# MLP input of a gMLP layer: the two transpositions left on TensorE go to VectorE, by k-tiles, from quadrants moved within SBUF

## The reference

```python
x = x + gmlp_mixer(rms_norm(x, norm1_g), a_w_in, a_ln_g, a_ws, a_bs, a_w_out)
x = x + channel_mlp(rms_norm(x, norm2_g), mlp_w1, mlp_w2)    # square(relu(h @ w1)) @ w2
return rms_norm(x, final_g)
```

## Time and profile before

| | |
|---|---|
| median of 3 runs | 1124.3 us (1124.18, 1124.3, 1125.67) |
| the profiled execution's own time | 1126.03 us |
| its span, first to last instruction | 1124.2 us |
| PE busy | 1114.8 us, 5088 matmuls |
| DVE busy | 785.9 us, 833 instructions |
| ACT busy | 569.4 us, 870 instructions |
| POOL busy | 23.5 us |
| mean granted clock of PE | 0.998 |
| DMA | 193.80 MB, mean 172 GB/s |

### The profile page before, as it was taken

How to read it: one execution, slowest core, us unless ns; L and a number is a source line. 1 busy time by engine, 2 the same in 40 slices (tenths; PEclk the granted TensorE clock), 3 DMA queues, 4 the chain that set the end, 5 groups by cost and what they waited for, 6 DMA issues and landing times.

```text
span 1124.2 us, 13090 instructions
## 1 busy us (share of the span) xinstructions
PE 1114.8 (99%) x5088; PEld 928.2 (83%) x5088; DVE 785.9 (70%) x833; ACT 569.4 (51%) x870; POOL 23.5 (2%) x17
## 2 busy tenths in 40 slices
PE   8999999999999999999999999999999999999997
PEld 7888888888888888888888888888888888888886
DVE  4976655688779986678658547455599575677666
ACT  6774444553554334565774365454653433433456
POOL 0000000000000000000000000000000000000240
PEclk9999999999999999999999999999999999999999
DMA  8173253272865494731353635527878354343213
GB/s 294 45 210 127 94 187 113 75 244 93 316 250 221 159 358 144 217 113 38 113 187 126 211 113 183 193 108 272 293 292 305 111 226 187 113 150 113 78 73 150
DMA packets 81933, 193.80 MB, mean 172 GB/s; under 512 B 4528, under 2 KB 10704, under 8 KB 75216
## 3 DMA queue, kind: packets, MB, share of 16 engines
q1 hardware_dynamic: 81392, 192.69, 48.7%
q10 hardware_dynamic: 480, 0.28, 0.1%
HBM read 134.24 MB, written 58.72 MB: 172 GB/s over the span
## 4 chain that ended last, share of the span: by engine, by line
PE 98%; DMA 1%; ACT 0%; DVE 0%; ACTq 0%; issue 0%
PE banks L427 32%; PE banks L432 32%; PE banks L431 32%; PE banks L496 3%; PE banks L541 1%; DMA gain_rows<-in_a_ln_g_dram 1%; DVE rows L1516 0%; ACT spare L1133 0%; PE banks L503 0%; PE banks L552 0%; PE banks L523 0%; ACT rows L1325 0%; ACT o_rms L1333 0%; ACTq L922 0%; ACTq L924 0%
## 5 line engine op out<-in xcount | busy, mean ns | idle before, releaser
L984 ACT ACTIVATE pair_high<-left_and_right 128x1024 fp32r<-128x1024 f32 x168 | 177.2, 1060 | 244.4 <-PE banks L427 193.4
L1378 DVE TENSOR_TENSOR ring_low<-left_and_right,ring_high 128x512 fp32r<-128x512 f32 x224 | 152.6, 692 | 192.7 <-ACT ring_high L954 192.3
L1386 DVE TENSOR_TENSOR pair_low<-left_and_right,pair_high 128x1024 fp32r<-128x1024 f32 x168 | 204.1, 1230 | 113.9 <-ACT pair_high L984 113.9
L954 ACT ACTIVATE ring_high<-left_and_right 128x512 fp32r<-128x512 f32 x224 | 138.4, 629 | 251.2 <-PE banks L427 155.9
L427 PE MATMUL banks<-pair_high 128*128 128x512 f32 x672 | 261.9, 390 | 0.0
L432 PE MATMUL banks<-pair_high,pair_low 128*128 128x512 f32 x672 | 261.5, 389 | 0.0
L431 PE MATMUL banks<-pair_low,pair_high 128*128 128x512 f32 x672 | 261.4, 389 | 0.0
L427 PE MATMUL banks<-s_high,ring_high 128*128 128x512 f32 x384 | 149.6, 389 | 0.0
L431 PE MATMUL banks<-s_low,ring_high 128*128 128x512 f32 x384 | 149.4, 389 | 0.0
L432 PE MATMUL banks<-s_high,ring_low 128*128 128x512 f32 x384 | 149.4, 389 | 0.0
L427 PEld LDWEIGHTS banks<-pair_high 128*128 128x128 f32 x672 | 126.1, 188 | 26.6 <-DVE pair_low L1386 0.3
(11 more groups left out here) (116 smaller groups left out, 1223.5 us busy)
## 6 DMA issues: line engine op xcount, KB each, us to landing
left_and_right<-sums SPq DMA_DIRECT2D x40, 1024.0 KB, 7.1
left_and_right<-in_mlp_w_dram SPq DMA_DIRECT2D x36, 1024.0 KB, 6.5
sums<-rows SPq DMA_DIRECT2D x34, 1024.0 KB, 5.4
left_and_right<-in_a_w_in_dram SPq DMA_DIRECT2D x19, 1024.0 KB, 6.2
v_blocks<-rows SPq DMA_DIRECT2D x8, 1024.0 KB, 4.5
left_and_right<-in_a_w_out_dram SPq DMA_DIRECT2D x8, 1024.0 KB, 9.7
rows<-in_x_dram SPq DMA_DIRECT2D x7, 1024.0 KB, 8.7
spare<-v_blocks SPq DMA_DIRECT2D x6, 1024.0 KB, 6.9
```

The source lines that it names most:

```text
L954: nc.scalar.activation(ring_high[k][:, :], right_place(n, pos)[:, k, :], ACT.Copy)\
L984: nc.scalar.activation(pair_high[pair_entry(d, pos, k)][:, :, :], pair_of(d, pos, k), ACT.Copy)\
L1378: nc.vector.tensor_tensor(ring_low[k][:, :], right_place(n, pos)[:, k, :], ring_high[k][:, :].bitcast(F32), ALU.subtract).then_inc(low_don ...
L1386: nc.vector.tensor_tensor(pair_low[e][:, :, :], pair_of(d, pos, k), pair_high[e][:, :, :].bitcast(F32), ALU.subtract).then_inc(low_done, 1)
```

## The change

All four blocks of y are turned by DVE.

- **a12 and a22** are no longer turned by PE (32 transpositions and 8 evictions by ACT go). Once y's block is final, `move_quads` moves it within SBUF into the quadrant layout, in 16 DMAs of 64 KB, without going through DRAM: for a12 all 16 on SP's queue, for a22 8 on SP's and 8 on ACT's. In SP's list the 16 stand ahead of the store of c11 and the load of w1's block b12.
- **`turn_y`** turns one k-tile (512 elements) per instruction, four per block, 16 in all. DVE turns a21 at the head of double 0's position 6, a12 behind its k = 7 and between the first splits of single 4, and a22 between the splits of positions 1 and 2 of single 4.
- **s3 and s2** (and s4) are made by k-tiles: `sum_turned`, a scalar_tensor_tensor that multiplies by the gain at the same time. ACT's separate scaling of a21 goes; that of a11 stays, by k-tiles. a12 and a22 are scaled while their high and low parts are written (`high_turned`, `low_turned`).
- **PE** waits per unit, not per block, for a12, s2 and a22 of single 4 (`STEPPED`).
- **`add_rows(0, 6)`**, which makes c21 final, stands ahead of the third split of single 4's position 0 instead of behind the fourth.
- **Gains:** only a_ln_g is still turned on PE, in single 1 at position 2 beside `turn_ws`; norm2_g comes in fours for both halves (w1's rows too), and a negated copy is made by DVE. Both loads leave ACT's queue at the start and go on SP's behind the first weights.

```diff
+STEPPED = {0: [], 4: ["a11", "a12", "s2", "a22"]}
...
+        def move_quads(eng, b, blk, dst, quadrants):
+            for q in quadrants:
+                for r in range(4):
+                    eng.dma_start(dst[32 * q:32 * q + 32, r:4 * QT:4, :],
+                                  block_of[blk][32 * r:32 * r + 32, :, P * q:P * q + P]).then_inc(quads_landed[b], 16)
...
@@ PE, single_unit
-                    if pos == 0:
-                        pe.wait_ge(combo_low, (10 if n == 4 else 0) + k + 1)
+                    if pos == 0 and n == 0:
+                        pe.wait_ge(combo_low, k + 1)
+                    elif s in STEPPED[n]:
+                        pe.wait_ge(combo_low, combo_count(n, s, k))
                     elif k == 0:
-                        pe.wait_ge(combo_low, combo_low_count(n, s))
+                        pe.wait_ge(combo_low, combo_count(n, s))
@@ PE, single and double
-                        if n == 4 and pos == 0 and k == 1:
-                            turn(4, "a22", set_of(slot(4, 1)))
                         if pos == 2 and k == 2 and n == 1:
+                            turn_gains()
                             turn_ws()
-                        if d == 0 and pos == 6 and k == 5:
-                            turn(4, "a12", set_of(slot_double(0, 5)))
-            turn_gains()
             warm(3)
@@ SP, double(0)
+                    sp.wait_ge(low_done, unit_double(0, 5, 7) + 1)
                     y_final(sp, "c11")
+                    move_quads(sp, "a12", "c11", quad_a12, range(4))
                     sp.dma_start(y_of("c11"), block_of["c11"]).then_inc(y_stored["c11"], 16)
...
                     y_final(sp, "c21")
+                    sp.wait_ge(low_done, unit_double(0, 6, 7) + 1)
+                    move_quads(sp, "a22", "c21", quad_a22, (0, 1))
                     sp.dma_start(y_of("c21"), block_of["c21"]).then_inc(y_stored["c21"], 16)
@@ ACT, single(4)
-                    high_combo(4, "a12")
+                    high_turned("a12")
                     split_high(4, 1, 0)
-                    evict_turned(4, "a22", set_of(slot(4, 1)))
+                    y_final(act, "c21")
+                    act.wait_ge(low_done, unit_double(0, 6, 7) + 1)
+                    move_quads(act, "a22", "c21", quad_a22, (2, 3))
                     split_high(4, 1, 1)
@@ DVE
+            def turn_y(blk, steps=range(4)):
...
+                for j in steps:
+                    nc.vector.transpose(dst[:, j, :], src[:, :, j:P:4]).then_inc(y_turned, 1)
```

More of the change, by code:

```diff
@@ L291, in trunk @@
         g2_landed = sem("g2_landed")
-        quads_landed = {b: sem(f"quads_landed_{b}") for b in ("a11", "a21", "a12")}
+        quads_landed = {b: sem(f"quads_landed_{b}") for b in ("a11", "a21", "a12", "a22")}
         y_turned = sem("y_turned")
         y_scaled = sem("y_scaled")
+        g2_negated = sem("g2_negated")
         v_stored = {b: sem(f"v_stored_{b}") for b in BLOCKS}
@@ L562, in single @@
                         if n == 0 and pos == 0 and k > 0:
-                            turn(0, {1: "a12", 2: "a21", 3: "a22"}[k], set_of(1))
-                        if n == 4 and pos == 0 and k == 1:
-                            turn(4, "a22", set_of(slot(4, 1)))
+                            turn({1: "a12", 2: "a21", 3: "a22"}[k], set_of(1))
                         if pos == 2 and k == 2 and n == 1:
+                            turn_gains()
                             turn_ws()
@@ L1312, in _ @@
             first_high(3)
[L1313 removed]
+            evict_turned("a11", set_of(1))
             for n in range(4):
@@ L1447, in low_a11, with low_turned @@
                                         ALU.subtract).then_inc(combo_low, 1)
+            def low_turned(s):
+                for k in range(4):
+                    dve.wait_ge(combo_high, combo_count(4, s, k))
+                    nc.vector.scalar_tensor_tensor(out=low[s][:, k, :], in0=raw_of[s][:, k, :],
+                                                   scalar=g2_fours[:, 0, k:k + 1],
+                                                   in1=high[s][:, k, :].bitcast(F32), op0=ALU.mult, op1=ALU.subtract)\
+                      .then_inc(combo_low, 1)
@@ L1452, in low_combo @@
                                         ALU.subtract).then_inc(combo_low, 1)
[L1454 to L1457 removed]
+            def turn_y(blk, steps=range(4)):
+                src, dst = {"a11": (quad_a11, raw_a11), "a21": (quad_a21, raw_a21), "a12": (quad_a12, raw_a12),
+                            "a22": (quad_a22, raw_a22)}[blk]
+                dve.wait_ge(quads_landed[blk], 64 if blk in ("a11", "a21") else 256)
@@ L1619, in single @@
                 elif n == 4:
-                    add_rows(0, 6)
-                    low_combo(4, "a12")
+                    low_turned("a12")
+                    split_low(4, 1, 0)
                     sum_t(4, 0)
-                    split_low(4, 1, 0)
                     split_low(4, 1, 1)
-                    sum_combo(4, "s2")
+                    for k in range(2):
+                        turn_y("a22", [k])
+                        sum_turned("s2", [k])
                     split_low(4, 1, 2)
@@ L1819, in double @@
                         turn_y("a11")
+                    if d == 0 and pos == 6:
+                        turn_y("a21")
                     for k in range(4, 8):
@@ L1839, in double @@
                     if pos == 6 and d == 0:
-                        sum_combo(4, "s3")
+                        turn_y("a12", [0, 1, 2])
                     for k in range(4):
+                        if pos == 6 and d == 0 and k == 1:
+                            turn_y("a12", [3])
+                        if pos == 6 and d == 0 and k == 2:
+                            add_rows(0, 6)
                         if pos < 6 or d == 1:
```

211 lines of the change are left out of this document (120 added, 91 removed).

## The result

The changed kernel takes 1128.88 us in the median of 7 runs (1127.95 to 1129.61), the kernel before 1124.65 in the runs beside it: ratio 1.0035, with a 95% interval of 1.0025 to 1.0044. It is **slower by 4.2 us**, and outside the range. The profiled execution took 1128.88 with a span of 1126.7, against 1126.03 and 1124.2 before.

A forecast was written before the change was run, and what follows sets the result against it. PE, busy 1114.8 of 1124.2 us, was taken to bound the kernel. Turns -3.56, stalls +5.2, start -0.74 and gains' transposition +0.2 gave +1.1 us: median 1125.4, range 1120.6 to 1128.4.

The forecast's parts named there:

- The turns: PE around single 4: removing two turns of 16 transpositions saves 3.56 us, 1.78 per turn.
- DVE's list: DVE from 485.91 to s1's low part: 52.9 us of work, ending at 538.9 without waits, about 543.0 with them.
- ACT's order and DVE's wait for it: Single 4, position 2: ACT writes unit k = 2's high part behind `snap`, by 533.7; DVE waits 2.9 us.
- The landing: a22's quadrants: moves issued until 513.5 and 513.9, landed at about 517.0; DVE asks at 516.6 and waits 0.4 us.
- The stalls: PE in single 4: 5.2 us of stalls against 3.56 saved, position 3 starting at about 543.0 instead of 537.8.
- and only behind it stands `snap`: ACT's list: `snap` follows the high part of s2's last k-tile, takes 2.18 us and delays position 2's k = 2.
- Three pieces: PE's stalls in single 4: small at 505, 2 us at 532, 3 at 540.
- The clock: Rivals: PE's clock stays up at the start, 1123.7, chance 0.12; stalls at 532 to 543 lower it, 1127.1, chance 0.06.
- The start: First product at 8.75 instead of 9.49, -0.74 us; the gains' transposition returns in single 1, +0.2.
- Keeping up: Rival: a k-tile's turn costs DVE 0.60 us rather than 0.99, so DVE is quick enough: 1120.7, chance 0.18.
- Late quadrants: Rival: a22's moves land at 520.3, 3.3 us later, and DVE's work from 516.6 follows one for one: 1128.7, chance 0.15.
- The Trainium skill's rule that gives a 128 x 128 transposition to TensorE: Sign against the change: by this rule the turns stay on PE and the change buys nothing.

The follow-up runs named there:

- experiment 4: The changed kernel with a22 turned by TensorE again, s2 summed in one operation and its high part written whole; a12 still turned by DVE: 1122.82 us, ratio 0.9983.
- 3: The changed kernel with a22's quadrants moved from c11 instead of c21, all on SP's queue, ACT issuing none (only its times count): 1128.39 us, ratio 1.0036.
- 5: The changed kernel with single 4's `snap` behind s2's third k-tile, ahead of its fourth: 1129.32 us, ratio 1.0040.
- Experiment 1: The changed kernel with single 4's `snap` of position 0 moved ahead of s2's third k-tile: 1125.75 us, ratio 1.0016.
- experiment 7: Experiment 1's kernel with all 16 moves of a22 on SP's queue and none on ACT's: 1130.56 us, ratio 1.0047.
- 8: Experiment 1's kernel with a12 turned by TensorE again and a22 still turned by DVE: 1128.31 us, ratio 1.0033.
- 9: Experiment 1's kernel with c21's 1 MB store held back on SP until all 16 moves of a22 have landed: 1126.22 us, ratio 1.0014.
- 10: The kernel with early `snap`, a12 turned by TensorE and a22 by DVE, plus c21's store held back until a22's moves have landed: 1125.00 us, ratio 1.0006.
- experiment 2: The kernel before with only the gains' part: loads on SP's queue, their transposition in single 1: 1124.28 us, ratio 0.9998.
- 6: Experiment 1's kernel with s1 made and split by k-tiles, and splits of positions 2 and 3 ahead of them: 1126.03 us, ratio 1.0012.

## Why the prediction was wrong

*The turns.* 3.56 us of PE time went, as said; experiment 4 finds one turn's 1.78 nearly whole.

*DVE's list* was right. It had s1's low part end at 543.1; it ended at 541.79, with everything 1.7 us earlier by the start. The k-tile of a turn, estimated at 0.99 us, has a pitch of 0.98 in a21's four together. a22's first turn was put at 517.0 and came at 515.12, 516.8 with the start taken out. ACT's order and DVE's wait for it (2.9 predicted, 2.56 measured) were right as well. Eight executions bear the list out: from a22's first turn to the end of s1's low part it takes 26.6 to 26.7 us with `snap` late (the change, 3, 5) and 24.7 to 24.8 with `snap` early (1, 7, 8, 9, 10).

*The landing.* Right in the sum, wrong in its terms: an issue costs 0.65 us on SP's queue (16 in 10.41) and 0.69 on ACT's (8 in 5.55), not 0.48, and a move lands 2.1 us later, not 3.3 as for a12 or 3.1 behind a22's last issue (513.9 to 517.0).

*The stalls.* 5.2 us predicted, 5.25 measured. That they agree is partly luck, since they are not the same stalls. **The step that failed is their place**, in the sentence "and only behind it stands `snap`": I charged `snap` with the 2.2 us by which it delays the next high part, for unit k = 2 of position 2, and never asked who waits for `snap` itself. Position 2 reuses position 0's banks, so its first unit was already held. Three pieces (0.3, 2 and 3 us, the longest at 540) became 0.34 at position 0 and one of 4.9 at position 2.

*The clock.* This is why the place mattered. The single stall of 4.75 us brought the clock down for some 7 us, 4.3 of them with PE at work, and 2.1 us were lost; the prediction gave a fall in the stalls a chance of 0.06 and a price of 1.7. DVE's list hides a little of it, so that 1.86 us reach position 3. Experiment 1, whose stalls come in smaller pieces, has no fall in its profile. The Trainium skill (TensorE: Matmul & The Clock Gate, The HAM clock gate), named in the prediction for just this case, has the idle PE throttled; the trace agrees, for waits of 2.58, 3.71, 4.75 and 5.33 us. With the place right, the case would have been the likeliest one: 1125.4 + 1.9 = 1127.3.

*The start.* The profile has it all: first product at 8.74 (8.75 predicted), clock 1.00 from 8 to 14 us. In the median it brought nothing that shows (experiment 2, between 1.2 us faster and 0.7 slower), where the sum had -0.54. What it may have taken away is the tail: the 27 runs of before beside experiment 2 go up to 1126.41, those of experiment 2 to 1124.82.

In sum 1127.3 + 0.5 = 1127.8. DVE's list was 0.4 longer than reckoned (541.79 against 543.1 - 1.7), and the kernel before took 1124.65 in the runs beside the change, where the forecast started from 1124.3: 1128.6. The last 0.3 to the measured 1128.88 stays open, and is within the scatter. Runs of kernels that move a22 within SBUF scatter by 1.7 to 5.8 us, those of e2 and e4 by 1.1.

*The rivals.* Keeping up fell by the k-tile's 0.98 us. Late quadrants was the right time, 1128.7, by the wrong mechanism: a22 landed on time in the changed kernel. It is real all the same, as experiments 5, 7 and 8 show. The Trainium skill's rule that gives a 128 x 128 transposition to TensorE (VectorE: DVE Perf Modes, Rules for kernel authors) held for a22 and not for a12, whose turns DVE had time for (4).

## What to carry to other kernels

When a step is moved on an engine that drains accumulators, ask who waits for its buffers, and not only what stands behind it in its own list. An engine that is 70% busy over the whole can still bound the kernel for 25 us, from the landing of the last input on, and then reordering its list mostly chooses which consumer waits. Take work off that stretch: turning a22 on PE did it (4), turning a12 on PE, whose work lies ahead of it, did not (10). If waits can't be avoided, several short ones were cheaper here than one long one that TensorE's clock followed down.

## What the runs showed of the hardware

The same wait of 2.1 us at position 3 was followed by the clock of 1.2 GHz in two profiled executions (experiments 7 and 9) and not in four others (1, 5, 8, 10), nor was one of 2.21 us at position 4 (6). The four longer ones in single 4 (2.58, 3.71, 4.75 and 5.33 us) all were. Where DVE was late anyway, the fall cost nothing: in experiment 7 the one after 523.73 left position 3 later by 3.3 us, the landing's delay and no more. The one behind position 3 cost 1.6.

One queue can hold up the other's transfers. With the store of 1 MB held back, the 16 moves of 64 KB land within 2.2 us each (10). With it issued on SP's queue ahead of ACT's last moves, the longest landing was 4.7 us (8), and 4.8 in 5 with the same order. Landings of 3.2 us came without it as well (1, 9).
